# Diagonal blocks gathered by VectorE and carried by one store, the block load issued alone, SiLU in the third chunk, the inverse at later places

## The reference

```
a_mat = where(strict, einsum('bhncd,bhnsd->bhncs', k_beta, k) * decay, 0)
t_mat = triangular_solve(eye + a_mat, eye, lower=True)
u = t_mat @ (v * beta);  w = t_mat @ (k_beta * exp(g))
v_new = u - w @ s;  o = q_dec @ s + qk @ v_new;  s = s * gt + k_dec.T @ v_new
```

## Time and profile before

| | |
|---|---|
| median of 3 runs | 1247.62 us (1246.43 to 1248.07) |
| the profiled execution's own time | 1249.48 us |
| its span, first to last instruction | 1247.7 us |
| granted TensorE clock, mean | 0.970 |
| TensorE busy | 1149.6 us (92%) |
| VectorE, ScalarE, GpSimd busy | 52%, 41%, 16% |
| gain and shift of one tile on GpSimd (L733, L737), 8 pieces | 5.6 us |
| `silu` on ScalarE, two table loads and four activations | 5.2 us |

### The profile page before, as it was taken

How to read it: one execution, slowest core, us unless ns; L and a number is a source line. 1 busy time by engine, 2 the same in 40 slices (tenths; PEclk the granted TensorE clock), 3 DMA queues, 4 the chain that set the end, 5 groups by cost and what they waited for, 6 DMA issues and landing times. The chain is left out here.

```text
span 1247.7 us, 19748 instructions
## 1 busy us (share of the span) xinstructions
PE 1149.6 (92%) x7340; PEld 900.9 (72%) x7340; DVE 650.1 (52%) x1996; ACT 505.5 (41%) x1475; POOL 198.0 (16%) x268
## 2 busy tenths in 40 slices
PE   4988989888999999999999999999899989899997
PEld 2766767666777868786786878777686868687776
DVE  3345554645355464646356364745437363636565
ACT  3363636363352625353352433336233534353220
POOL 4522323122210101023000101012100000000340
PEclk9998989898999999999999999999999999999999
DMA  6753745545572543632436362625244343522232
GB/s 212 287 191 123 252 164 161 179 136 153 161 237 102 164 160 104 211 127 78 150 132 193 124 192 79 201 84 172 85 165 157 110 137 110 168 79 61 94 109 84
DMA packets 63887, 183.57 MB, mean 147 GB/s; under 512 B 16240, under 2 KB 28976, under 8 KB 50480
## 3 DMA queue, kind: packets, MB, share of 16 engines
q1 hardware_dynamic: 63792, 182.32, 44.1%
HBM read 138.22 MB, written 44.07 MB: 146 GB/s over the span
## 5 line engine op out<-in xcount | busy, mean ns | idle before, releaser
L760 PE MATMUL bank<-xr,w 128*128 128x512 f32 x2496 | 684.8, 414 | 5.1 <-ACT conv_in L1091 3.2
L760 PEld LDWEIGHTS bank<-xr,w 128*128 128x128 f32 x2496 | 455.5, 193 | 108.5 <-issue 14.8
L733 POOL TENSOR_TENSOR x_tile<-x_tile,gain 128x256 f32<-128x256 f32 x40 | 28.1, 736 | 716.6 <-DVE x_tile L1484 716.6
L810 PE MATMUL bank<-wo,y_split 128*128 128x512 f32 x432 | 118.8, 409 | 0.0
L810 PEld LDWEIGHTS bank<-wo,y_split 128*128 128x128 f32 x432 | 76.2, 188 | 17.1 <-issue 1.9
L1410 DVE SCALAR_TENSOR_TENSOR kq<-conv_in,convw_all,kq 128x512 f32<-128x512 f32 x96 | 76.5, 796 | 3.4
L1332 ACT ACTIVATE blocks<-bank 128x128 f32<-128x128 f32 x64 | 17.8, 277 | 149.0 <-PE bank L1027 148.8
L1605 DVE TENSOR_TENSOR y_step<-blocks,y_cols 128x60 f32<-128x60 f32 (+14 forms) x240 | 49.7, 207 | 49.7 <-DMA blocks<-n_spill 42.0
L1227 ACT ACTIVATE score<-score,neg_max 128x256 f32<-128x256 f32 (+1 forms) x128 | 62.5, 490 | 16.8 <-DVE neg_max L1572 16.8
L1297 ACT ACTIVATE blocks<-bank 128x256 f32<-128x256 f32 (+1 forms) x64 | 24.4, 382 | 105.1 <-PE bank L974 73.7
L1692 DVE SCALAR_TENSOR_TENSOR t<-bank,cols_all,v_tok 128x128 f32<-128x128 f32 x64 | 22.3, 348 | 84.8 <-PE bank L1012 84.8
(11 more groups left out here) (214 smaller groups left out, 1762.1 us busy)
## 6 DMA issues: line engine op xcount, KB each, us to landing
w<-w_split SPq DMA_DIRECT2D x78, 1024.0 KB, 5.0
w_split<-w SPq DMA_DIRECT2D x26, 1024.0 KB, 4.9
blocks<-n_spill SPq DMA_DIRECT2D x16, 512.0 KB
y_spill<-y_out SPq DMA_DIRECT2D x30, 256.0 KB, 6.3
y_tile<-w_in SPq DMA_DIRECT2D x13, 512.0 KB, 6.1
x_tile<-w_in SPq DMA_DIRECT2D x13, 512.0 KB, 6.2
y_tile<-y_spill SPq DMA_DIRECT2D x12, 512.0 KB, 6.7
x_tile<-x SPq DMA_DIRECT2D x12, 512.0 KB, 5.6
```

The costliest lines, as they stand in the source:

```text
L733: nc.gpsimd.tensor_tensor(res[:, part], res[:, part], gain[:, part], ALU.mult).then_inc(scaled.sem, 1)
L760: ins = nc.tensor.matmul(bank[at % 2][:], w[:, turn % 3, wp, k, :], xr[:, xp, k], start=(step == 0), stop=(step == 3 * KT - 1))
L810: ins = nc.tensor.matmul(bank[at % 2][:], y_place(t)[:, yp, k], wo[:, k, wp, half * UNIT:(half + 1) * UNIT], start=(step == 0), stop=(step ...
```

## The change

`base_inverses` now reads its blocks from a buffer in which the row of the block comes before the chunk; the numbers are the same. The blocks reach it in another way: VectorE multiplies n_t by a mask of the partition's own block (`own_block`) into `pt`, and adds up the eight column blocks into `y_step`, 64 numbers in each partition. One DMA stores that. The block load comes right behind the store, ahead of the decay load, and SP issues nothing more (but the decay load) until it has landed. The output transposes (with v's) move from place 0.13 to 0.16. The six inverse places and the chunks move later by 0.005 to 0.02 of a slot. The order of o1 and bz is exchanged in slots 4 to 6 and 8 to 10. ScalarE takes exp of the decay row before k's squares, SiLU in chunk 2 where its gate inputs are there, and holds the last `w_hi` of slots 0 and 1 until q's squares of the next slot are done. `split_y` of a tile moves from chunk 2 to chunk 3.

```diff
@@ names_in
     if s == 1 or s == 2:
-        return ["q", "k", "v", "z", "o0", "o1", "bz", "bq"]
+        return ["q", "k", "v", "z", "o0", "bz", "o1", "bq"]
@@
-AT_SCORES0, AT_VTOK, AT_TURNS0, AT_VALUES0 = 0.09, 0.13, 0.24, 0.31
+AT_SCORES0, AT_VTOK, AT_TURNS0, AT_VALUES0 = 0.09, 0.16, 0.24, 0.31
@@ Places
-        first = 0.47 if short else 0.36 if long else 0.42
+        first = 0.49 if short else 0.375 if long else 0.44
-        self.step0, self.step = (0.665, 0.082) if short else (0.6, 0.097) if long else (0.62, 0.092)
+        self.step0, self.step = (0.685, 0.077) if short else (0.605, 0.096) if long else (0.635, 0.088)
@@
-        blocks = sb("blocks", [P, CH, BASE * BASE])
+        blocks = sb("blocks", [P, BASE, CH, BASE])
@@ SP
             def store_blocks(n):
-                after(sp, n_ready, n, CH)
-                for g in range(P // BASE):
-                    part = slice(g * BASE, (g + 1) * BASE)
-                    sp.dma_start(n_spill[n, g].rearrange("t a c -> a t c"), n_t[part, :, part]).then_inc(n_stored.sem, 16)
+                after(sp, picked, n, 2)
+                sp.dma_start(n_spill[n], y_step[:].rearrange("p t c -> p (t c)")).then_inc(n_stored.sem, 16)
             def load_blocks(n):
-                after(sp, n_stored, n, 16 * (P // BASE))
+                after(sp, n_stored, n, 16)
                 after(sp, ot_done, n - 1, 1)
-                source = n_spill[n].rearrange("g t a c -> g (t a c)").unsqueeze(1)\
+                source = n_spill[n].rearrange("(g a) m -> g (a m)", a=BASE).unsqueeze(1)\
                     .to_broadcast([P // BASE, BASE, CH * BASE * BASE])
@@ SP, slot
                 store_blocks(n)
+                load_blocks(n)
                 if i < AH - 1:
                     after(sp, pt_ready, n, 2)
                     load_decay(n + 1)
+                after(sp, blocks_in, n, 16)
                 if i == AH - 1 and 0 < s < SBS - 1:
                     after(sp, x_low_dve, s + 1, 1)
                     load_x(s + 1, 3)
-                load_blocks(n)
                 after_jobs(n, 0.16)
@@ ACT
                 if at in W_AT and W_AT[at] + 3 < TILES_W:
-                    w_hi(W_AT[at] + 3)
+                    if at + 1 < len(JOBS) and JOBS[at + 1].n > max(job.n, -1) >= 0:
+                        held.append(W_AT[at] + 3)
+                    else:
+                        w_hi(W_AT[at] + 3)
@@ ACT, slot: L1253 to L1255 move ahead of L1245; after the squares of q:
+                split_weight()
@@
-                after_jobs(n, at.step0)
+                after_jobs(n, min(at.step0, 0.66))
                 copy_turned(n, 1)
+                silu_before = CH - 2 if silu_at(n) - n < at.chunk(CH - 2) and n < SLOTS - 1 else CH - 1
                 for c in range(CH):
+                    if c == silu_before:
+                        after_jobs(n, max(at.chunk(c), silu_at(n) - n))
+                        if c < CH - 1:
+                            silu(n, True)
...
@@ DVE, base_inverses
-                    nc.vector.tensor_tensor(y_step[:, :, rest], blocks[:, :, j * BASE + j + 1:(j + 1) * BASE],
+                    nc.vector.tensor_tensor(y_step[:, :, rest], blocks[:, j, :, j + 1:],
@@ DVE, slot, behind n_t (L1643)
+                after(dve, n_ready, n, CH)
+                wide = [P, CH, P // BASE, BASE]
+                nc.vector.tensor_tensor(pt[:].rearrange("p t (b c) -> p t b c", c=BASE),
+                                        n_t[:].rearrange("p t (b c) -> p t b c", c=BASE),
+                                        own_block[:].unsqueeze(1).unsqueeze(3).to_broadcast(wide), ALU.mult)\
+                    .then_inc(picked.sem, 1)
+                after(dve, picked, n, 1)
+                nc.vector.tensor_reduce(y_step[:], pt[:].rearrange("p t (b c) -> p t c b", c=BASE), AXIS.X, ALU.add)\
+                    .then_inc(picked.sem, 1)
+                after(dve, picked, n, 2)
                 after(dve, qtok_done, n, 1)
@@ DVE, chunks
-                    if c == 2:
+                    if c == CH - 1:
                         if t is not None and i == AH - 2:
                             split_y(t + 1)
```

More of the change, by code:

```diff
@@ L267, in build_layer @@
         eg_row = v_tok
-        blocks = sb("blocks", [P, CH, BASE * BASE])
-        shared = blocks[:].rearrange("p t n -> p (t n)")
+        blocks = sb("blocks", [P, BASE, CH, BASE])
+        shared = blocks[:].rearrange("p j t c -> p (j t c)")
         def quarter(a):
@@ L404, in build_layer @@
         v_tok_ready = counter("v_tok_ready", CH)
-        n_stored = counter("n_stored", 16 * (P // BASE))
+        picked = counter("picked", 2)
+        n_stored = counter("n_stored", 16)
         blocks_in = counter("blocks_in", 16)
@@ L1110, in _, with split_weight @@
             place = [0]
+            held = []
+            def split_weight():
+                while held:
+                    w_hi(held.pop())
             def after_job(at):
@@ L1244, in slot @@
                 at = Places(n)
+                after(act, g_row_in, n, 16)
+                after(act, resid_ready, n - 1, CH)
+                nc.scalar.activation(eg_row[:], decay[:], ACT.Exp).then_inc(eg_ready.sem, 1)
                 after(act, ktok_done, n, 1)
@@ L1252, in slot @@
                 nc.scalar.activation(r_k[:], ln_ss[:, 0], ACT.Exp, scale=-0.5).then_inc(rk_ready.sem, 1)
-                after(act, g_row_in, n, 16)
-                after(act, resid_ready, n - 1, CH)
-                nc.scalar.activation(eg_row[:], decay[:], ACT.Exp).then_inc(eg_ready.sem, 1)
                 if i == 0:
@@ L1328, in slot @@
                             round_y(15)
-                        silu(n, True)
+                        if silu_before == c:
+                            silu(n, True)
                     after_jobs(n, at.chunk(c, 2 / 3))
```

9 lines of the change are left out of this document (6 added, 3 removed).

## The result

The change makes the kernel slower: 1261.67 us (median of 4 runs, 1259.74 to 1266.1) against 1247.15 (4 runs of before beside them), a ratio of 1.0115 with a 95% interval of 1.0095 to 1.0134. I had predicted 1220. The profiled execution has a span of 1259.7 us, 12.0 more than before.

A forecast was written before the change was run, and what follows sets the result against it. TensorE was taken as the bound, its largest idle part waiting for y0 (44.8 us), with the clock adding. 13.3 + 17.7 - 3.8 = 27.2 us off 1249.48 gave 1222.3, with the runs' median 1.9 lower: 1220 predicted, range 1203 to 1239.

The forecast's parts named there:

- Slots 4 to 11: The middle slots: late weights, x loads and late norm outweigh the gains; together 3.8 us lost.
- 4, 8: Slots 4 and 8: y0 waits of 2.7 and 2.4 us plus clock fall to 1.1 each; 6.3 us gained.
- 5, 9: Slots 5 and 9: blocks at 22, weight load at 27.3, so 3.8 us wait plus 1.7 each; 6.4 us lost.
- 6, 10: Slots 6 and 10: losses of 0.7 and 1.4 us become 1.7 each; 1.3 us lost.
- 7, 11: Slots 7 and 11: the next unit's x load comes late, 4.2 us wait plus 1.7 each; 3.6 us lost.
- Slots 0 to 3: First slots: earlier y0, later places and better clock gain 2.1, 4.4, 4.4 and 2.4 us, together 13.3.
- the standard slot: Slot 6: the block load also waits for ot_done, moved from 0.13 to 0.16, six steps or 1.3 us later.
- Slots 12 to 15: Last slots: 22.9 us lost to waits and clock before, 5.2 kept; 17.7 us gained.
- SiLU in chunk 2 hidden: ScalarE: SiLU's 5.2 us leave the slot's end and hide behind jobs in the new place.
- The gather: VectorE, ahead of the softmax and inverses: 1.4 us with two waits on itself (0.95 to 2.2), reduction taken as 0.68.
- The block load alone: Block load with other transfers held back: 6.6 to 7.5 us, landing at about 19, inverses starting where they did.
- slower: Rival: TensorE waits for z's weights, deciding at 7.0 us lost per slot in slots 4 to 11; 1256 us, chance 0.08.

The follow-up runs named there:

- r7_vtok: Changed kernel with the old job order, without SP's wait for the block load, and with the output transposes back at 0.13: 0.9882 of the kernel before, 1228.97 us.
- f1_store: Changed kernel with a tile's output in slots 5, 6, 9 and 10 issued behind the next slot's block load: 1.0074 of the kernel before.
- c1_both: Kernel before plus the gather with one store and ScalarE's edits; load order, job order and places as before: 0.9906 of the kernel before.
- c2_wait: Kernel before plus the gather with one store, the block load ahead of the decay load and SP's wait for its landing: 1.0063 of the kernel before.
- r2_free: Changed kernel without SP's wait for the landing of the block load, which stays ahead of the decay load: 1.0073 of the kernel before.
- r6_order_free: Changed kernel with the job order of before and without SP's wait for the block load: 0.9960 of the kernel before.
- r1_order: Changed kernel with o1 ahead of bz again in slots 4 to 6 and 8 to 10, nothing else: 1.0043 of the kernel before.
- c3_order: Kernel before plus the gather with one store, o1 behind bz in slots 4 to 6 and 8 to 10, split_y in chunk 3: 1.0169 of the kernel before.

## Why the prediction was wrong

The sum was 13.3 + 17.7 - 3.8 = 27.2 us won. By the slots above it was 5.0 + 9.5 - 26.0 = -11.5 us, a loss (with the 0.5 us by which slot 0 begins later, the 12.0 us between the spans).

**Slots 4 to 11: -26.0 instead of -3.8.** This is the step that failed, and with it the sign: the price of the late queue and the late norm in these slots. By pairs (waits of TensorE in one slot, without the 1.0 us for copies, conv_in, that slots 7 and 11 had before too):

| slots | predicted | measured | waits predicted, each | measured |
|---|---|---|---|---|
| 4, 8 | +6.3 | +0.2 | 1.1 | 2.8, 3.4 |
| 5, 9 | -6.4 | -11.5 | 3.8 | 5.9, 6.4 |
| 6, 10 | -1.3 | -11.0 | 1.7 | 5.8, 5.2 |
| 7, 11 | -3.6 | -3.7 | 4.2 | 4.0, 4.2 |

The mechanism was the one I described: SP held at the tile's output, the block store behind 2.5 MB, the weights behind the blocks. In slots 5 and 9 its size was right too: the blocks come at 23.3 and 24.4, not 22, and the weights cost 3.8 and 5.0 us. What I left out are two other waits in the same slots. I priced what TensorE itself asks of SP, the weights, and not what ScalarE asks of it: the load of the y tile goes out behind the weights, ScalarE's order puts its split in front of the copy of t0, and L969 takes 9.8 us in five waits where I had none. And I took n_t at its old time, while GpSimd's 5.6 us now lie beside VectorE's operations; with the gather that gives 1.3 to 1.4 us at the softmax in slots 5, 6, 9 and 10, where r7_vtok, with the gather and the old order, waits nothing. (Slot 4 waits 1.5 us for it too, but there n_t ends at 8.9 as before, and the gather alone does it.) In slots 6 and 10 the copy and the softmax together are 4.8 and 3.7 of 5.8 and 5.2 us. The waits make 16 of the 22 us between forecast and result. The rest is mostly the clock. I had it low in slots 5, 7, 9 and 11 only. In the trace slots 6, 8 and 10 have a granted clock of 0.98 too (6 and 10 stood at 1.00 before), and slot 9 has 0.95. In slot 8 the longest wait is 1.96 us, shorter than the 2.3 us from which I had counted a wait as long, and TensorE ran at the lower level right behind it (0.50 from 681 to 684 us). For slots 7 and 11 the sum is right and its content is not: the x load was in time, and TensorE waits for two copies of ScalarE instead (za at L811, score at L896). There the agreement is luck.

**Slots 0 to 3: 5.0 instead of 13.3.** Slots 1 and 2 won 3.8 and 5.4 (predicted 4.4 each), slot 0 0.6 (2.1). The waits did not fall here in sum: y0 fell from 18.2 to 9.9 us, but L1019 (5.7), the softmax (5.5) and `pre` took its place, and what these slots won is mostly the clock (0.96 instead of 0.92). That share is uncertain: slot 0 of f1_store has the same four waits, a granted clock of 0.90 instead of 0.97, and takes 66.9 us instead of 62.8, though its edit begins only in slot 5. Slot 3 lost 4.8 where I had a gain of 2.4. The block load also waits for the output transposes; I worked this out for the standard slot as 1.3 us, and gave slot 3 nothing for it, though its place counts 263 steps. The load left at 17.4 instead of 15.6. r7_vtok, with the place back, agrees: it loads at 15.4, and TensorE waits 10.3 us in the slot instead of 12.3. A wait of 2.7 us for `pre` (L795) is new in this slot and had no term. It is not the transposes': r7_vtok keeps 2.6 of it, and c1_both, with the old places of the inverse and the chunks, has none.

**Slots 12 to 15: 9.5 instead of 17.7.** Slots 13 and 14 won 3.6 and 4.7. The waits at L963 fell from 12.6 to 0.6, more than I said. The terms that were too small are the softmax, 2.0 to 2.1 us in slots 12 to 14 where I had 1.4 in two of them and 0.9 in slot 12, and L1019, which waits 1.31 us for a copy of ScalarE in each of three slots (and 5.7 in slots 0 to 2). I had called SiLU in chunk 2 hidden; 9.7 us of it are not. Slot 12 also falls to the lower clock (0.97) behind a wait of 2.10 us, where I had no long wait left; slots 13 and 14, with 2.04, stay at 1.00.

**The gather** was 1.8 us and not 1.4, since the reduction took 1.04 where I took 0.68; within my bounds, 2.2.

**What held.** The block load alone takes about 7.1 us in slot 6, as said. The rule of the Trainium skill ("DMA: Bandwidth & Descriptors", "Rules for kernel authors") that a DMA is spread over at most as many engines as its outermost dimension has elements spoke against holding the others back. c2_wait agrees in its result, a loss of 1.6%, but not wholly in the step between: I had said that the load alone gains nothing, and it brings the inverses of slot 6 forward by 1.1 us. L948's waits are gone. L761 waits for w 12.8 us, 8.8 of it in slots 5 and 9. SP stands for GpSimd 134.0 us instead of 58.5:

```profile
SPq L576 <- POOL x_tile L738: 134.0, 8, 23.2
...
SPq L505 <- DMA blocks<-n_spill: 41.5, 7, 6.2
```

The clock rose to 0.976, not 0.98. From the two spans and clocks (1259.7 us at 0.976, 1247.7 at 0.970) I estimate some 60 us at the lower level instead of 75.

**The rivals.** The rival "slower" named TensorE's wait for z's weights, 7.0 us a slot as the point where it decides. Slots 4 to 11 lose 49.4 us now (23.4 + 26.0), 6.2 each. That was enough because the rest won 14.5 and not 32.2. The weights are 12.8 us of it. So that rival had the sign and the place, and about a quarter of the amount; its 0.08 was far too small, since the terms left out above (the copy behind the y tile, n_t beside GpSimd, the clock) all point the same way as it does.

**What stays open.** The parts don't add up. The order costs 0.7% in the whole change, 1.0 with the rest of the cost gone, 1.1 without the wait (r2_free to r6_order_free) and 2.7 on the gather alone; the wait costs 0.4, 0.8 (r1_order to r6_order_free) and 1.6. Both hold one queue, so that either covers part of the other; f1_store shows this for one pair, and I haven't shown it for the rest. Held w_hi, exp's place and the inverse's places were not tried by themselves, and which of them brings the wait for `pre` in slot 3 is open.

## What to carry to other kernels

When an edit holds an in-order DMA queue, list every transfer behind the point, and for each the engine that stands for it and what is next in that engine's order: here a copy queued behind a late y tile cost TensorE 9.8 us in slots 4 to 11, beside 12.8 for the weights themselves, and in c2_wait and f1_store it cost far more than they did. A store that waits for a slow engine belongs behind the small transfers that others wait for, not in front of them; that edit alone took c3_order from 1.0169 to 0.9986, but gave only 0.4% where another wait held the same queue. When a transfer is put off, look in the old trace at how long its reader already stood for it: a reader that comes free just in time has nothing to give. And a place counted in work is longer in a slot with more work: price a moved place in the longest slot as well.
